# Mixture-of-experts stage: plain activations gathered, norm applied on gathered rows and products, nineteen weight places instead of sixteen

## The chip, the cores and the metric

The kernel runs on one core of a Trainium2 chip. The metric is the device time of one execution in microseconds (us); lower is better. TensorE (PE) multiplies matrices, VectorE (DVE) and ScalarE (ACT) work element by element, GpSimd (POOL) issues the gathers and scatters with indices, and SyncE (SP) issues the plain transfers.

## What is computed

The program is a network of three layers on 512 tokens of width 1024, all in float32. The change lies in the last stage, a mixture of experts: each token goes to two of 32 experts.

```python
h2 = rms_norm_2(x, g_ffn[l])
x = x + hier_moe(h2, ...)

def rms_norm_2(x, g):
    y = xf * lax.rsqrt(jnp.mean(xf * xf, axis=-1, keepdims=True) + EPS)
    return (y * g.astype(jnp.float32)).astype(x.dtype)

def hier_moe(h, wg, bg, we, be, w1, w3, w2):
    pg = softmax(hf @ wg + bg)           # 4 groups, the best one is taken
    le = (hf @ we + be)                  # 8 experts in it, the best two are taken
    ...
    def expert_block(args):
        xb, e = args
        return (jax.nn.silu(xb @ w1[e]) * (xb @ w3[e])) @ w2[e]
    ...
    ys = ys * gate_buf[:, None]
    out = zeros.at[tok_buf].add(ys)
```

`w1` and `w3` of an expert are 1024 x 512 each, `w2` is 512 x 1024: 6 MB for an expert, 192 MB for all of them. The root of a token's mean square is one number for a token, the gain `g_ffn` one number for a feature.

## The kernel before

The activations `x` and the normed `um` lie with features on partitions (8 tiles of 128 x 512). The stage needs rows of tokens, so it goes like this.

**Head.** While the last projection of the attention (`CH_2O`, lines 548 to 576) still runs, `act_sum` scales `x` by `g_ffn` into `um` on ACT (L1132). `pe_route` multiplies `um` by the router's weights (L2403) and sums the squares (L2399), PE turns `um` to token order (L2366), and ACT copies the turned tiles out with the token's root as scale (L2541). SP stores those rows to DRAM (`h_tokens`, L2336). DVE works out the routing (`dve_route`); for each expert `dve_slots` makes a 0/1 matrix (L2601), `pe_meta` multiplies it by a table of token numbers and gates (L2431), and `dve_indices` turns the result into indices (L2611 to L2613). Three experts' indices are made ahead (`AHEAD`).

**One round of the loop over experts.** PE's order is written out in `pe_expert(e)`: the up products of expert e (L2458, 16 matmuls of the program, which the profile shows as 32), the turn of the hidden rows of expert e-1 (L2490), the turn of the gathered rows of expert e+1 (`pe_x_turn`, L2450), the meta product of expert e+3 (L2431), the down products of expert e-1 (L2466). ACT works out the sigmoid in three steps (L2553 to L2557), copies the turned hidden rows (L2560), copies the turned gathered rows out of their bank (`act_gathered`, L2582) and scales the expert's output by its gate (L2590). DVE multiplies (L2631, L2633), makes the slots of expert e+3 (L2601), multiplies by the sigmoid (L2640), and makes the indices. POOL gathers the rows of expert e+3 when the turned bank lets it, and scatters the outputs. Each engine runs its own list in order; semaphores join them.

In rounds 4 to 7 PE also turns `x` itself to token order (`pe_tokens`, L2420) and ACT copies it out (`act_tokens`): the experts' outputs are added to it at the end.

**Weights.** An expert has six pieces of 128 x 2048 (1 MB). SP loads them in the order of use into 16 places (`SLOTS`). A piece can be issued when the piece 16 before it has been used (`w_used`). Nine places are free while the last projection runs; seven (`LATE`) lie where the ring of dense weights and other tiles are, and the last two are loaded behind the stores of `h_tokens`. After the last scatter but before the last two pieces SP loads the scattered pairs back (L2353), and the last three experts' outputs are put in place by products (`pe_last`, L2524; `dve_last`, L2676).

Of the kernel before, what the change touches and what calls it, by code (L numbers as in the profile page):

```python
# [36 lines left out]
SLOTS = 16  # L37
LAST = 3
LATE = 7
# [1059 lines left out]
def scalar_program(k):  # L1099
    act, s = k.act, k.s  # L1100
    k.nc.scalar.preload_act_table_set("natural_log_exp_and_others")
    act.wait_ge(s["gains_in"], 16)
    for j in range(4):
        act.wait_ge(s[f"x_in{j}"], 16)
        act_inputs(k, k.u, "g_a0", (2 * j, 2 * j + 1))
        for i in range(2):
            act_square_sum(k, 0, 2 * j + i, 2 * j + i)
    act.wait_ge(s["eps_ready"], 2)
    act_project(k, CH_AB, N_AB, k.y, lambda: act_root(k, "norm_a0", k.ch7, k.ch7.bank, k.rs, D))
    act_ab_prepare(k)  # L1110
# [12 lines left out]
    act_da(k)  # L1123
    act_sb(k)
    act_sum(k, CH_2O, 5, k.um, "g_ffn")
# [1094 lines left out]
def moe_buffers(k):  # L2220
    s = k.s
    k.dense.close()
    s.new("router_in", *(f"w_in{j}" for j in range(SLOTS) if j >= len(W_IN) and not 0 <= j - SLOTS + LATE < RING))
    s.new("routed", "route_shifted", "route_exp")
    s.new("h_turned", "h_copied0", "h_copied1", "h_stored", "x_turned", "x_copied0", "x_copied1")
# [17 lines left out]
    k.mt = [k.sb(f"mt{j}", [P, 4]) for j in range(2 * SETS)]  # L2243
# [12 lines left out]
    k.rtok = k.small[:, 480:496]  # L2256

# [36 lines left out]
W_IN = ("x_in0", "x_in1", "x_in2", "x_in3", "cmp_k_in", "cmp_v_in", "tables_in")  # L2294
# [6 lines left out]
def piece_in(k, j):  # L2301

    late = j - SLOTS + LATE
    if 0 <= late < RING:
# [16 lines left out]
def moe_sync(k):  # L2321
    sp, s = k.sp, k.s
    sp.wait_ge(s["o_normed"], 8)
    sp.dma_start(k.wr, k.t["router"]).then_inc(s["router_in"], 16)
    for g, (e, i) in enumerate(ORDER):
        if g == PAIRS_AT:
# [29 lines left out]
def moe_tensor(k):  # L2356
    pe, s = k.pe, k.s
    pe_route(k)
    for b in range(NB):
        for h in range(2):  # L2360
# [4 lines left out]
            for kk in range(4):  # L2365
                ins = pe.transpose(k.bank[4 + 2 * (b % 2) + h][:, kk * P:(kk + 1) * P], k.um[:, 4 * h + kk, b * P:(b + 1) * P], k.const("ident"))  # L2366
# [19 lines left out]
def pe_route(k):  # L2386
# [3 lines left out]
    pe.wait_ge(s["router_in"], 16)  # L2390
    for kk in range(KT):
        if kk == 0:
            pe.wait_ge(s["combined"], 2 * (N_CH // 2 - 1))
            pe.wait_ge(s["u_ready"], 46)
        if kk == KT - 2:
# [5 lines left out]
            pe.wait_ge(s["u_ready"], 48)  # L2401
        for b in range(NB):
            ins = pe.matmul(k.bank[b][:, 0:NG + NE], k.um[:, kk, b * P:(b + 1) * P], k.wr[:, kk, :], start=kk == 0, stop=kk == KT - 1)  # L2403
# [5 lines left out]
AHEAD, X_TURN = 3, 4  # L2409
TOKEN_BANKS = (3, 6)  # L2410


def pe_tokens(k, b):

    pe, s = k.pe, k.s
    for h in range(2):
        if b:
            pe.wait_ge(s[f"x_copied{h}"], b)
        for kk in range(4):
            ins = pe.transpose(k.bank[TOKEN_BANKS[h]][:, kk * P:(kk + 1) * P], k.x[:, 4 * h + kk, b * P:(b + 1) * P], k.const("ident"))  # L2420
        ins.then_inc(s["x_turned"], 1)


def pe_meta(k, e):
# [103 lines left out]
def moe_scalar(k):  # L2528
# [3 lines left out]
    act.wait_ge(s["root_ready"], k.root_at["norm_ffn"])  # L2532
    for b in range(NB):
# [5 lines left out]
        for h in range(2):  # L2539
            act.wait_ge(s["h_turned"], 2 * b + h + 1)  # L2540
            act.activation(k.htok[b][:, h * T:(h + 1) * T], k.bank[4 + 2 * (b % 2) + h], ACT.Copy,  # L2541
                           scale=k.rtok[:, 4 * b:4 * b + 1]).then_inc(s[f"h_copied{h}"], 1)
    act.wait_ge(s["h_stored"], 16 * NB)
    half = EH // 2
    sig = k.sig[:, 0:half]
    for e in range(NE + 1):
        if e == 0:
            act_gathered(k, 0)
        if e < NE:
            act.wait_ge(s["w_used"], up_used(e))  # L2550
            if e:
                act.wait_ge(s["hid_done"], e)
            act.activation(sig, k.bank[2][:, 0:half], ACT.Exp, scale=-1.0).then_inc(s["sig_exp"], 1)  # L2553
# [7 lines left out]
        if e + 1 < NE:  # L2561
            act_gathered(k, e + 1)
        if e:
            act_out(k, e - 1)
        if 0 <= e - X_TURN < NB:
            act_tokens(k, e - X_TURN)


def act_tokens(k, b):
    act, s = k.act, k.s  # L2570
    for h in range(2):
        act.wait_ge(s["x_turned"], 2 * b + h + 1)
        act.copy(k.xtok[:, b, h * T:(h + 1) * T], k.bank[TOKEN_BANKS[h]]).then_inc(s[f"x_copied{h}"], 1)

# [30 lines left out]
def dve_indices(k, e):  # L2605
# [5 lines left out]
    dve.wait_ge(own.sem, own.link(dve.tensor_copy(mt, k.bank[7][:, 0:4])))  # L2611
    dve.wait_ge(own.sem, own.link(dve.tensor_scalar(mt[:, 3:4], mt[:, 3:4], -4.0 * T, k.const("half_far"), ALU.mult, ALU.add)))
    dve.tensor_scalar(idx, mt[:, 0:2], 2.0, mt[:, 3:4], ALU.mult, ALU.add).then_inc(s["idx_ready"], 1)  # L2613
# [5 lines left out]
def moe_vector(k):  # L2619
# [5 lines left out]
    dve_count(k)  # L2625
    for e in range(NE):
# [16 lines left out]
        if e == NE - 2:  # L2643
            dve.wait_ge(s["x_copied0"], NB)
            dve.wait_ge(s["x_copied1"], NB)
# [42 lines left out]
def dve_route(k):  # L2688
# [19 lines left out]
    own.link(dve.memset(k.meta[:, :, :, 3], 1.0))  # L2708
# [57 lines left out]
def moe_pool(k):  # L2766
    pool, s = k.pool, k.s
    pool.wait_ge(s["zeroed"], 64)
# [25 lines left out]
def fallback(k, e, c):  # L2794
# [19 lines left out]
    gates = own.link(dve.tensor_copy(mt, k.bank[7][:, 0:4]))  # L2814
# [11 lines left out]
    act.wait_ge(s["f_pe"], done.link(ins))  # L2826
    act.copy(xT.rearrange("p c a t -> p (c a t)"), k.bank[0]).then_inc(s["f_act"], 1)
    pe.wait_ge(s["f_act"], 1)
# [3 lines left out]
    act.activation(sig, k.bank[2][:, 0:half], ACT.Exp, scale=-1.0).then_inc(s["f_act"], 1)  # L2832
    act.wait_ge(s["f_act"], 2)
    act.activation(sig, sig, ACT.Ln, bias=1.0).then_inc(s["f_act"], 1)
    act.wait_ge(s["f_act"], 3)
    act.activation(sig, sig, ACT.Exp, scale=-1.0).then_inc(s["f_act"], 1)
    dve.wait_ge(s["f_act"], 4)
    dve.wait_ge(own.sem, own.link(dve.tensor_tensor(k.prod, sig, k.bank[2][:, 0:half], ALU.mult)))
    hid = own.link(dve.tensor_tensor(hN, k.prod, k.bank[2][:, half:EH], ALU.mult))
# [5 lines left out]
    pe.wait_ge(s["f_act"], 5)  # L2845
# [41 lines left out]
```

## Time and profile before

| | |
|---|---|
| time, median of 3 runs | 2402.06 us |
| lowest and highest run | 2401.61 and 2406.68 us |
| span of the profiled execution | 2390.3 us |
| PE busy | 2240.4 us (94%) |
| DVE busy | 1375.2 us (58%) |
| ACT busy | 563.7 us (24%) |
| mean granted TensorE clock | 0.967 of full |

The span runs from the first to the last instruction of the profiled execution; the time of a run also holds what lies around it, some 11.8 us by the median. The stage of the experts begins with the first up product at 1888.4 us of the span. Its weights are read at some 418 GB/s, and PE is busy for some 91% of it. An engine's busy share says little here, since PE and the transfers both run nearly without a break; one has to see which of the two the other waits for.

### The profile page before, as it was taken

To read this page: it belongs to the slowest core of one execution; us is meant where nothing else is said; L and a number is where in the kernel's file an instruction comes from. 1 tells how busy PE (TensorE), PEld (TensorE's weight loads), DVE (VectorE), ACT (ScalarE), POOL (GpSimd) and SP (SyncE) were. 2 spreads that over 40 slices of the span, in tenths; PEclk is the share of its full clock that TensorE was granted. 3 is DMA by queue.
4 is the path that set the end of the run, shared out by engine and by line. 5 is a ranking of instruction groups with operands and counts; after the bars stand their busy time and mean duration, and the time that the engine had idled before them with its cause. 6 is when DMAs were issued, how large, how long until landed. Compare 5 with 4: busy or idle time off the path is not lost.

```text
span 2390.3 us, 29072 instructions
## 1 busy us (share of the span) xinstructions
PE 2240.4 (94%) x10734; PEld 1630.0 (68%) x10734; DVE 1375.2 (58%) x3525; ACT 563.7 (24%) x1375; POOL 64.7 (3%) x65
## 2 busy tenths in 40 slices
PE   8988889999999998999999999999799899899987
PEld 6864568888888885558888888888557533333332
DVE  6559857666566657996665666765776311211114
ACT  2013342100011205772100010301583211211110
POOL 0000000000000000000000000000000011111110
PEclk9998799999999999999999999999899799999999
DMA  5220022222323320002332222333004799999997
GB/s 201 88 80 7 17 72 73 87 87 88 88 89 88 126 64 25 1 1 71 88 87 86 85 88 85 100 88 88 1 1 179 276 418 414 418 417 417 418 418 297
DMA packets 69885, 348.11 MB, mean 146 GB/s; under 512 B 10852, under 2 KB 11748, under 8 KB 44208
## 3 DMA queue, kind: packets, MB, share of 16 engines
q1 hardware_dynamic: 64576, 337.13, 38.9%
q0 software_dynamic: 4880, 8.05, 0.9%
q8 instruction: 88, 1.44, 0.2%
q10 hardware_dynamic: 288, 1.05, 0.1%
q14 instruction: 53, 0.43, 0.1%
HBM read 341.00 MB, written 17.30 MB: 150 GB/s over the span
## 4 chain that ended last, share of the span: by engine, by line
PE 71%; DVE 8%; DMA 4%; ACT 3%; issue 2%; DVEq 0%; SPq 0%; ACTq 0%
PE bank L557 26%; PE bank L2458 8%; PE bank L562 7%; PE bank L576 7%; PE bank L569 7%; PE bank L2466 5%; DMA w<-in_experts 4%; PE bank L548 2%; PE bank L2431 1%; DVE exps L1806 1%; PE bank L889 1%; DVE square L2601 1%; PE bank L876 1%; PE bank L901 1%; DVE exps L1996 1%
## 5 line engine op out<-in xcount | busy, mean ns | idle before, releaser
L2458 PE MATMUL bank<-w,xT 128*64 128x512 f32 x960 | 215.6, 598 | 5.7 <-DMA w<-in_experts 4.9
L2631 DVE COPY square<-bank 128x256 f32<-128x256 f32 x32 | 13.6, 425 | 353.1 <-ACT rope L2553 353.1
L2458 PEld LDWEIGHTS bank<-w,xT 128*64 128x64 f32 x960 | 68.3, 138 | 145.4 <-issue 133.1
L1302 ACT ACTIVATE exps<-exps,small 128x128 f32<-128x128 f32 (+1 forms) x224 | 124.3, 559 | 100.2 <-DVE small L1806 99.7
L557 PE MATMUL bank<-u,ring 128*128 128x256 f32 x608 | 143.7, 379 | 0.0
L1576 DVE TENSOR_TENSOR third<-first,bank 128x256 f32<-128x256 f32 x108 | 45.5, 421 | 170.6 <-PE bank L557 169.8
L2466 PE MATMUL bank<-w,square 128*64 128x512 f32 x480 | 131.1, 695 | 5.8 <-ACT square L2560 2.9
L557 PEld LDWEIGHTS bank<-u,ring 128*128 128x128 f32 x608 | 115.4, 190 | 16.5 <-issue 1.0
L557 PE MATMUL bank<-h,ring 128*128 128x256 f32 x512 | 120.9, 379 | 0.0
L557 PE MATMUL bank<-h_sums,w_sum 128*128 128x256 f32 x512 | 120.9, 379 | 0.0
L557 PE MATMUL bank<-u_mlp_sums,w_sum 128*128 128x256 f32 x480 | 113.4, 379 | 0.0
L557 PE MATMUL bank<-u_mlp,ring 128*128 128x256 f32 x480 | 113.4, 379 | 0.0
L557 PE MATMUL bank<-exps,w_sum 128*128 128x256 f32 x464 | 109.6, 379 | 0.0
L557 PEld LDWEIGHTS bank<-h,ring 128*128 128x128 f32 x512 | 97.3, 190 | 13.2
L557 PEld LDWEIGHTS bank<-h_sums,w_sum 128*128 128x128 f32 x512 | 97.3, 190 | 13.2
L1243 ACT ACTIVATE h<-relu 128x512 f32<-128x512 f32 x64 | 40.3, 630 | 274.1 <-DVE relu L1721 249.3
L557 PEld LDWEIGHTS bank<-u_mlp,ring 128*128 128x128 f32 x480 | 91.2, 190 | 12.4
L557 PEld LDWEIGHTS bank<-u_mlp_sums,w_sum 128*128 128x128 f32 x480 | 91.2, 190 | 12.4
L557 PEld LDWEIGHTS bank<-exps,w_sum 128*128 128x128 f32 x464 | 88.2, 190 | 12.0
L2790 POOL DMA_INDIRECT x_gathered<-h_tokens,idx x32 | 35.3, 1103 | 2080.3 <-DVE idx L2613 1881.1
L2466 PEld LDWEIGHTS bank<-w,square 128*64 128x64 f32 x480 | 36.8, 157 | 75.8 <-issue 69.6
L2431 PE MATMUL bank<-sums,square 128*128 128x4 f32 x256 | 37.9, 271 | 48.7 <-DVE square L2601 48.7
(442 smaller groups left out, 4228.4 us busy)
## 6 DMA issues: line engine op xcount, KB each, us to landing
w<-in_experts SPq DMA_DIRECT2D x180, 1024.0 KB, 21.1
ring<-in_dense SPq DMA_DIRECT2D x216, 512.0 KB, 3.7
consts<-in_experts SPq DMA_DIRECT2D x12, 1024.0 KB
w<-y_pairs SPq DMA_DIRECT2D x4, 1024.0 KB, 26.8
consts<-in_consts SPq DMA_DIRECT2D x1, 2310.5 KB, 16.5
x<-in_xT SPq DMA_DIRECT2D x4, 512.0 KB, 8.0
h_tokens<-u SPq DMA_DIRECT2D x4, 512.0 KB, 2.8
bias_scratch<-y_ab SPq DMA_DIRECT2D x4, 320.0 KB, 2.4
```

What stands on the lines that cost most here:

```text
L548: ins = pe.matmul(bank, w[:, j, :], x(j), start=i == 0, stop=i == 3)
L557: ins = pe.matmul(bank, w[:, j, :], x(j), start=j == 0, stop=j == 3)
L562: ins = pe.matmul(part[2], a12[:, j, :], tile(2 * j + 1)[:, 0:HT], start=j == 0, stop=j == 3)
L569: ins = pe.matmul(part[4], a22[:, j, :], t4[:, j, :], start=j == 0, stop=j == 3)
L576: ins = pe.matmul(part[3], s4[:, j, :], tile(2 * j + 1)[:, HT:T], start=j == 0, stop=j == 3)
L1243: act.activation(k.hs[q % 2][:, j + a, :], k.rc[a], ACT.Square).then_inc(s["h_ready"], 1)
L1302: act.activation(e, e, ACT.Exp, bias=neg[:, a:a + 1], scale=-1.0, accum_out=total[:, a:a + 1]).then_inc(s[done], 1)
L1576: dve.tensor_tensor(u3, u2, part[7], ALU.add).then_inc(s["shared"], 1)
L2431: ins = pe.matmul(k.bank[7][:, 0:4], k.S[:, b, :], k.meta[:, b, e, :], start=b == 0, stop=b == NB - 1)
L2458: ins = k.pe.matmul(bank[a * CAP:(a + 1) * CAP, :], xT[:, kk % 4, kk // 4, :], w[:, (2 * (kk % 2) + a) * EH:(2 * (kk % 2) + a + 1) * EH], ...
L2466: ins = k.pe.matmul(bank[a * CAP:(a + 1) * CAP, :], hT[:, c % 2, c // 2, :], w[:, c % 2 * D + a * T:c % 2 * D + (a + 1) * T], start=c == 0 ...
L2790: k.pool.indirect_dma_start(k.xgat, None, k.hscr, bass.IndirectOffsetOnAxis(ap=k.idx[e % (2 * SETS)][:, 0:1].bitcast(U32), axis=0), bounds ...
```

## The change

The normed activations are no longer made. The router's weights are scaled by the gain instead, once, on POOL; the plain `x` is turned to token order, copied without a scale, stored and gathered. The gain is then applied by DVE when it copies the turned gathered rows out of their bank, and the root of each row by a scale on ACT and DVE where the products of the expert are read. The root comes with the row: the fourth column of the meta table, so far all ones, holds minus the root, and one more DVE instruction finds the empty slots. Since the plain rows now lie in token order from the start, the turns of `x` in rounds 4 to 7 go, and the tile `x` is free for weights behind the stores: two places. A third comes from halving the region where descriptors of POOL's transfers are kept (`SCRATCH`).

```diff
-SLOTS = 16
+SLOTS = 19
+EARLY, LATE = 12, 5
-LATE = 7
+SCRATCH = 8192
...
-    act_sum(k, CH_2O, 5, k.um, "g_ffn")
+    act_sum(k, CH_2O, 5, None, None)
...
-    late = list(range(SLOTS - LATE, SLOTS))
-    k.w = {j: k.sb(f"w{j}", [P, PIECE]) for j in late + list(range(SLOTS - LATE - 1))}
+    k.w = {j: k.sb(f"w{j}", [P, PIECE]) for j in [*range(EARLY, EARLY + LATE), *range(2, EARLY)]}
     done = k.cpack.at["swap"][0]
-    k.w[SLOTS - LATE - 1] = k.consts[:, done:done + PIECE]
+    k.w[1] = k.consts[:, done:done + PIECE]
+    for j in range(2):
+        k.w[EARLY + LATE + j] = k.x.rearrange("p k t -> p (k t)")[:, PIECE * j:PIECE * (j + 1)]
...
 def moe_sync(k):
     sp, s = k.sp, k.s
+    load_piece(k, *ORDER[0])
     sp.wait_ge(s["o_normed"], 8)
     sp.dma_start(k.wr, k.t["router"]).then_inc(s["router_in"], 16)
...
-        if g == SLOTS - LATE:
+        if g == EARLY:
             sp.wait_ge(s["prod_done"], 7 * N_CH // 2)
-        if g == SLOTS - 3:
+        if g == EARLY + LATE - 1:
             sp.wait_ge(s["combined"], N_CH)
-        if g == SLOTS - 2:
+        if g == EARLY + LATE:
...
     for e in range(NE + 1):
         pe_expert(k, e)
-        if 0 <= e - X_TURN < NB:
-            pe_tokens(k, e - X_TURN)
...
-            act.activation(sig, k.bank[2][:, 0:half], ACT.Exp, scale=-1.0).then_inc(s["sig_exp"], 1)
+            act.activation(sig, k.bank[2][:, 0:half], ACT.Exp, scale=minus_root(k, e)).then_inc(s["sig_exp"], 1)
...
-def act_gathered(k, e):
-    k.act.wait_ge(k.s["g_turned"], e + 1)
-    k.act.copy(k.xT[e % 2].rearrange("p c a t -> p (c a t)"), k.bank[0]).then_inc(k.s["g_copied"], 1)
+def dve_gathered(k, e):
+
+    gains = k.vec("g_ffn").rearrange("p (a c) -> p c a", a=2).unsqueeze(3).to_broadcast([P, 4, 2, CAP])
+    k.dve.wait_ge(k.s["g_turned"], e + 1)
+    k.dve.tensor_tensor(k.xT[e % 2], k.bank[0].rearrange("p (c a t) -> p c a t", c=4, a=2), gains, ALU.mult).then_inc(k.s["g_copied"], 1)
...
-    dve.wait_ge(own.sem, own.link(dve.tensor_scalar(mt[:, 3:4], mt[:, 3:4], -4.0 * T, k.const("half_far"), ALU.mult, ALU.add)))
-    dve.tensor_scalar(idx, mt[:, 0:2], 2.0, mt[:, 3:4], ALU.mult, ALU.add).then_inc(s["idx_ready"], 1)
+    dve.wait_ge(own.sem, own.link(dve.tensor_scalar(mt[:, 4:5], mt[:, 3:4], 0.0, -4.0 * T, ALU.is_lt, ALU.mult)))
+    dve.wait_ge(own.sem, own.link(dve.tensor_scalar(mt[:, 4:5], mt[:, 4:5], k.const("half_far"), None, ALU.add)))
+    dve.tensor_scalar(idx, mt[:, 0:2], 2.0, mt[:, 4:5], ALU.mult, ALU.add).then_inc(s["idx_ready"], 1)
...
+    dve_gathered(k, 0)
     for e in range(NE):
...
-        dve.tensor_copy(k.prod, k.bank[2][:, 0:half]).then_inc(s["taken"], 1)
+        dve.tensor_scalar(k.prod, k.bank[2][:, 0:half], minus_root(k, e), None, ALU.mult).then_inc(s["taken"], 1)
         dve.wait_ge(s["taken"], e + 1)
-        dve.tensor_tensor(k.prod, k.prod, k.bank[2][:, half:EH], ALU.mult).then_inc(s["both"], 1)
+        dve.scalar_tensor_tensor(k.prod, k.bank[2][:, half:EH], minus_root(k, e), k.prod, ALU.mult, ALU.mult).then_inc(s["both"], 1)
+        if e + 1 < NE:
+            dve_gathered(k, e + 1)
         if e + AHEAD < NE:
             dve_slots(k, e + AHEAD)
...
+    pool.wait_ge(s["router_in"], 16)
+    pool.tensor_tensor(k.wr, k.wr, k.vec("g_ffn").unsqueeze(2).to_broadcast([P, KT, NG + NE]), ALU.mult).then_inc(s["router_scaled"], 1)
```

The list of DVE, one round of the loop in the kernel before. `square_6` is the product, `square_7` the slots of expert e+3, `rope_9` the hidden rows, `mt` and `idx` the table row and the indices.

```order
2998 L2631 COPY square_6<-bank 128x256
2999 L2633 TENSOR_TENSOR square_6<-square_6,bank 128x256
3000 L2601 TENSOR_SCALAR square_7<-consts,pos 128x128 x4
3001 L2640 TENSOR_TENSOR rope_9<-square_6,rope_10 128x256
3002 L2611 COPY mt_98<-bank 128x4
3003 L2612 TENSOR_SCALAR mt_98<-mt_98,consts 128x1
3004 L2613 TENSOR_SCALAR idx_106<-mt_98 128x2
```

The same round in the changed kernel; `xT` are the turned gathered rows.

```order
3011 L2613 TENSOR_SCALAR square_6<-bank,mt_96 128x256
3012 L2615 SCALAR_TENSOR_TENSOR square_6<-bank,mt_96,square_6 128x256
3013 L2562 TENSOR_TENSOR xT_89<-bank,vecs 128x512
3014 L2581 TENSOR_SCALAR square_7<-consts,pos 128x128 x4
3015 L2624 TENSOR_TENSOR rope_9<-square_6,rope_10 128x256
3016 L2591 COPY mt_99<-bank 128x4
3017 L2592 TENSOR_SCALAR mt_99<-mt_99 128x1
3018 L2593 TENSOR_SCALAR mt_99<-mt_99,consts 128x1
3019 L2594 TENSOR_SCALAR idx_107<-mt_99 128x2
```

An operation of 512 elements a partition, so far ACT's, now stands on DVE between the second product and the slots, and the indices take four instructions instead of three.

The list of SP around the stores of `h_tokens` in the kernel before: the late places from `w_72` on, and behind the stores the last two before the places come round.

```order
260 L2312 DMA w_86<-in_experts 128x2048
261 L2312 DMA consts<-in_experts 128x2048
262 L2312 DMA w_72<-in_experts 128x2048
263 L2312 DMA w_73<-in_experts 128x2048
264 L2312 DMA w_74<-in_experts 128x2048
265 L2312 DMA w_75<-in_experts 128x2048
266 L2312 DMA w_76<-in_experts 128x2048
267 L2336 DMA h_tokens<-u 128x1024 x4
268 L2312 DMA w_77<-in_experts 128x2048
269 L2312 DMA w_78<-in_experts 128x2048
270 L2312 DMA w_79<-in_experts 128x2048
```

And in the changed kernel.

```order
263 L2315 DMA w_85<-in_experts 128x2048
264 L2315 DMA w_86<-in_experts 128x2048
265 L2315 DMA w_72<-in_experts 128x2048
266 L2315 DMA w_73<-in_experts 128x2048
267 L2315 DMA w_74<-in_experts 128x2048
268 L2315 DMA w_75<-in_experts 128x2048
269 L2315 DMA w_76<-in_experts 128x2048
270 L2342 DMA h_tokens<-u 128x1024 x4
271 L2315 DMA x<-in_experts 128x2048 x2
272 L2315 DMA w_131<-in_experts 128x2048
```

Twelve pieces instead of nine now stand ahead of the five late ones (`w_77` and `w_78` have moved up among them), and the two behind the stores go into `x`.

## Rows read from the trace of the kernel before

**Rows 1.** Stretches: busy PE, PEld, DVE, ACT, POOL (us); granted clock, DMA share, GB/s

```profile
1842.00:1855.00 13.00, 13.00 (x65) 11.50 (x63) 5.78 (x14) 3.32 (x6) 0.00 (x0) 1.00 0.09 38
...
1883.00:1891.00 8.00, 5.73 (x20) 3.45 (x22) 2.23 (x12) 0.58 (x1) 1.00 (x1) 0.50 0.12 32
...
2250.00:2360.00 110.00, 95.16 (x442) 35.85 (x442) 21.76 (x66) 18.18 (x42) 12.56 (x12) 0.97 1.01 418
```

**Rows 2.** Timeline of SP's transfers, the first behind the stores: start, length, engine, line

```profile
1874.06 23.76 SPq L2312 DMA_DIRECT2D w<-in_experts  x6
```

**Rows 3.** Timeline of PE late in the stage; in brackets idle time and releaser

```profile
2268.78 5.32 PE L2458 MATMUL bank<-w,xT 128*64 128x512 f32 x24
...
2276.38 0.44 PE L2490 MATMUL bank<-consts,rope 128*128 128x128 f32 x2
...
2283.70 3.60 PE L2458 MATMUL bank<-w,xT 128*64 128x512 f32 x16
...
2292.29 0.44 PE L2490 MATMUL bank<-consts,rope 128*128 128x128 f32 x2
...
2325.88 3.65 PE L2466 MATMUL bank<-w,square 128*64 128x512 f32 x16 [0.83 <-ACT square L2560]
...
2340.54 0.44 PE L2490 MATMUL bank<-consts,rope 128*128 128x128 f32 x2
...
2372.42 5.42 PE L2466 MATMUL bank<-w,square 128*64 128x512 f32 x16 [2.83 <-DMA w<-in_experts]
```

**Rows 4.** Timeline of one undisturbed round, from the end of its up products

```profile
2115.76 0.44 PE L2490 MATMUL bank<-consts,rope 128*128 128x128 f32 x2
...
2116.04 0.60 PE L2450 MATMUL bank<-consts,x_gathered 128*128 128x128 f32 x4
...
2116.85 0.42 DVE L2633 TENSOR_TENSOR square<-square,bank 128x256 f32<-128x256 f32 x1
...
2117.19 0.87 DVE L2601 TENSOR_SCALAR square<-consts,pos 128x128 f32<-128x128 f32 x4
2117.32 0.59 ACT L2582 COPY xT<-bank 128x512 f32<-128x512 f32 x1
...
2118.11 1.05 PE L2431 MATMUL bank<-sums,square 128*128 128x4 f32 x8 [1.48 <-DVE square L2601]
...
2119.10 3.65 PE L2466 MATMUL bank<-w,square 128*64 128x512 f32 x16
...
2122.58 7.04 PE L2458 MATMUL bank<-w,xT 128*64 128x512 f32 x32
2129.55 0.44 PE L2490 MATMUL bank<-consts,rope 128*128 128x128 f32 x2
```

**Rows 5.** Timeline of DVE, an operation of 512 elements and its successor

```profile
1795.57 0.68 DVE L2139 TENSOR_TENSOR y<-y 128x512 f32<-128x512 f32 x1
1796.17 0.68 DVE L2147 TENSOR_TENSOR y<-y,bank 128x512 f32<-128x512 f32 x1
```

**Rows 6.** The chain that ended last: start, length, what; down products and a token turn

```profile
1938.93 5.28 PE bank L2466 x16
1976.28 1.02 PE bank L2420 x8
2036.45 3.58 PE bank L2466 x16
2174.31 3.58 PE bank L2466 x16
2204.02 6.47 PE bank L2466 x16
```

**Rows 7.** Timeline ahead of the first up product: indices, count, copy

```profile
1886.99 0.21 DVE L2612 TENSOR_SCALAR mt<-mt,consts 128x1 f32<-128x1 f32 x1
1887.24 0.23 DVE L2613 TENSOR_SCALAR idx<-mt 128x2 int32<-128x2 f32 x1
...
1887.60 0.15 DVE L2763 CAST count<-col 128x1 int32<-128x1 f32 x1
```

More of the change, by code:

```diff
@@ L2222, in moe_buffers @@
     k.dense.close()
-    s.new("router_in", *(f"w_in{j}" for j in range(SLOTS) if j >= len(W_IN) and not 0 <= j - SLOTS + LATE < RING))
+    s.new("router_in", "router_scaled", *(f"w_in{j}" for j in range(len(W_IN), SLOTS) if not EARLY <= j < EARLY + LATE))
     s.new("routed", "route_shifted", "route_exp")
-    s.new("h_turned", "h_copied0", "h_copied1", "h_stored", "x_turned", "x_copied0", "x_copied1")
+    s.new("h_turned", "h_copied0", "h_copied1", "h_stored")
     s.new("counted_in", "counted", "count_ready")
@@ L2242, in moe_buffers @@
     k.oN = [k.sb(f"oN{j}", [P, D // 2]) for j in range(SETS)]
-    k.mt = [k.sb(f"mt{j}", [P, 4]) for j in range(2 * SETS)]
+    k.mt = [k.sb(f"mt{j}", [P, 5]) for j in range(2 * SETS)]
     k.idx = [k.sb(f"idx{j}", [P, 2], I32) for j in range(2 * SETS)]
@@ L2256, in moe_buffers @@
     k.rtok = k.small[:, 480:496]
+    k.w[0] = k.sb("w0", [P, PIECE])
 def moe(k):
@@ L2301, in piece_in @@
 def piece_in(k, j):
-    late = j - SLOTS + LATE
-    if 0 <= late < RING:
+    late = j - EARLY
+    if 0 <= late < LATE:
         return k.s[f"ring_in{late}"], 16 * ((N_CH - late + RING - 1) // RING)
@@ L2389, in pe_route @@
     pe, s, ch = k.pe, k.s, k.ch7
-    pe.wait_ge(s["router_in"], 16)
+    pe.wait_ge(s["router_scaled"], 1)
     for kk in range(KT):
@@ L2400, in pe_route @@
             ch.end(ins, "norm_ffn")
-            pe.wait_ge(s["u_ready"], 48)
+            pe.wait_ge(s["combined"], N_CH)
         for b in range(NB):
-            ins = pe.matmul(k.bank[b][:, 0:NG + NE], k.um[:, kk, b * P:(b + 1) * P], k.wr[:, kk, :], start=kk == 0, stop=kk == KT - 1)
+            ins = pe.matmul(k.bank[b][:, 0:NG + NE], k.x[:, kk, b * P:(b + 1) * P], k.wr[:, kk, :], start=kk == 0, stop=kk == KT - 1)
     ins.then_inc(s["routed"], 1)
[L2409 to L2421, printed above, removed]
+AHEAD = 3
 def pe_meta(k, e):
@@ L2540, in moe_scalar @@
             act.wait_ge(s["h_turned"], 2 * b + h + 1)
-            act.activation(k.htok[b][:, h * T:(h + 1) * T], k.bank[4 + 2 * (b % 2) + h], ACT.Copy,
-                           scale=k.rtok[:, 4 * b:4 * b + 1]).then_inc(s[f"h_copied{h}"], 1)
-    act.wait_ge(s["h_stored"], 16 * NB)
+            act.copy(k.htok[b][:, h * T:(h + 1) * T], k.bank[4 + 2 * (b % 2) + h]).then_inc(s[f"h_copied{h}"], 1)
     half = EH // 2
@@ L2707, in dve_route @@
     own.link(dve.tensor_copy(k.meta[:, :, :, 0], tok))
-    own.link(dve.memset(k.meta[:, :, :, 3], 1.0))
+    own.link(dve.tensor_scalar(k.meta[:, :, :, 3], k.rtok[:, 0:4 * NB:4].unsqueeze(2).to_broadcast([P, NB, NE]), -1.0, None, ALU.mult))
     dve.wait_ge(s["routed"], 1)
@@ L2813, in fallback @@
     dve.wait_ge(s["f_pe"], done.link(ins))
-    gates = own.link(dve.tensor_copy(mt, k.bank[7][:, 0:4]))
+    gates = own.link(dve.tensor_copy(mt[:, 0:4], k.bank[7][:, 0:4]))
     for b in range(NB):
@@ L2825, in fallback @@
                                 start=b == 0, stop=b == NB - 1)
-    act.wait_ge(s["f_pe"], done.link(ins))
-    act.copy(xT.rearrange("p c a t -> p (c a t)"), k.bank[0]).then_inc(s["f_act"], 1)
-    pe.wait_ge(s["f_act"], 1)
+    gains = k.vec("g_ffn").rearrange("p (a c) -> p c a", a=2).unsqueeze(3).to_broadcast([P, 4, 2, CAP])
+    dve.wait_ge(s["f_pe"], done.link(ins))
+    pe.wait_ge(s["f_dve"], own.link(dve.tensor_tensor(xT, k.bank[0].rearrange("p (c a t) -> p c a t", c=4, a=2), gains, ALU.mult)))
     for kk in range(KT):
@@ L2831, in fallback @@
     act.wait_ge(s["f_pe"], done.link(ins))
-    act.activation(sig, k.bank[2][:, 0:half], ACT.Exp, scale=-1.0).then_inc(s["f_act"], 1)
+    act.wait_ge(s["f_dve"], gates)
+    act.activation(sig, k.bank[2][:, 0:half], ACT.Exp, scale=mt[:, 3:4]).then_inc(s["f_act"], 1)
+    act.wait_ge(s["f_act"], 1)
+    act.activation(sig, sig, ACT.Ln, bias=1.0).then_inc(s["f_act"], 1)
     act.wait_ge(s["f_act"], 2)
-    act.activation(sig, sig, ACT.Ln, bias=1.0).then_inc(s["f_act"], 1)
-    act.wait_ge(s["f_act"], 3)
     act.activation(sig, sig, ACT.Exp, scale=-1.0).then_inc(s["f_act"], 1)
-    dve.wait_ge(s["f_act"], 4)
-    dve.wait_ge(own.sem, own.link(dve.tensor_tensor(k.prod, sig, k.bank[2][:, 0:half], ALU.mult)))
-    hid = own.link(dve.tensor_tensor(hN, k.prod, k.bank[2][:, half:EH], ALU.mult))
+    dve.wait_ge(s["f_act"], 3)
+    dve.wait_ge(own.sem, own.link(dve.scalar_tensor_tensor(k.prod, k.bank[2][:, 0:half], mt[:, 3:4], sig, ALU.mult, ALU.mult)))
+    hid = own.link(dve.scalar_tensor_tensor(hN, k.bank[2][:, half:EH], mt[:, 3:4], k.prod, ALU.mult, ALU.mult))
     pe.wait_ge(s["f_dve"], hid)
```

39 lines of the change are left out of this document (13 added, 26 removed).

## The prediction

> **What bounds the kernel now.** I read the stretches of time first [rows 1]. From the first experts to the end the transfers run without a break at 418 GB/s (DMA share 1.01), and in the same 110 us PE is busy for 95.16. So both are close to their limit, and the question is which waits for which. There are two paths through the stage, and the end is the later of them.
>
> The path of the transfers: a piece of 128 x 2048 float32 is 1.0486 MB, at 418 GB/s 2.51 us. The transfers can only run ahead as far as there are places. Before the first up product they stood still twice: from 1842 to 1855 the share is 0.09, all nine early places being full, and from 1883 to 1891 it is 0.12, all sixteen being full [rows 1].
>
> The path of PE: in an undisturbed round the up products begin at 2122.58 and end where the next turn begins, at 2129.55, after 6.97 us [rows 4]. A round that waits for weights shows as a longer stretch between those two. Late in the stage there are three: 2268.78 to 2276.38 is 7.60, so 0.63 lost; 2283.70 to 2292.29 is 8.59, so 1.62 lost; and the products that follow the down products begun at 2325.88 should start after 3.48 us (2119.10 to 2122.58 [rows 4]), at 2329.36, and end at 2340.54, 11.18 later, so 4.21 lost. The last down products wait 2.83 [rows 3]. Sum 9.3 us: without any wait for weights PE would have ended at 2390.3 - 9.3 = 2381.0. That is all the slack it has. Until some 2270 us the bound is PE, and only the last seven rounds see the transfers.
>
> **The change, part by part.** All sums are made against the profiled span of 2390.3 us; the median of the runs is 11.8 us above it, which I add at the end.
>
> *Three more places.* Three pieces that were read behind the first up product are now read in the pause from 1842 to 1855, which is long enough for three (7.5 us of 13), and the two behind the stores are issued at 1874.06 as before [rows 2], so that all nineteen are full when the first is used. The path of the transfers gets 3 x 2.51 = 7.5 us shorter.
>
> *No normed copy, no scale on the copy of the turned tiles.* ACT's work in the head shrinks. It gives nothing: the first gather waits for indices, which hang on the routing, not on ACT. The router's weights are scaled on POOL, which is idle there, some 30 us before they are read.
>
> *Ahead of the first up product.* The indices take one more instruction, 0.25 us each time (1886.99 to 1887.24 [rows 7]), and three experts' indices are made in a row there: 0.75. The gathered rows used to be copied by ACT at 1887.80; now DVE does it behind the count, which ends at 1887.75, plus 0.75 is 1888.50, plus 0.68 for 512 elements [rows 5] is 1889.2. The first up product, at 1888.44 before, starts 0.8 later. Both paths carry that.
>
> *One round.* This is the term that matters. In the round shown, PE turns the gathered rows from 2116.04 to 2116.64 and then stands idle for 1.48 us, because the meta product needs the slots, which DVE makes from 2117.19 to 2118.06, behind its two products. ACT's copy of the gathered rows, 0.59 us from 2117.32 on, lies beside that and costs nothing [rows 4]. In the changed kernel DVE does this copy itself, in front of the slots. Its input is there (2116.64) before the second product ends (2117.27), so nothing hides it: slots, meta product, down products and next up products all move by one DVE operation of 512 elements. The distance from such an operation to the next one is 0.60 us, its own length 0.68 [rows 5]; I take 0.60, with 0.68 for the range. Below zero it cannot go, since an operation is added in front and none of DVE's goes; the two products only change their form. Of the 32 rounds 29 make slots: 29 x 0.60 = 17.4 us (19.7 at 0.68). The fourth index instruction falls beside the down products and costs nothing, and so does the hidden product (L2640), which is late by 0.6 but has the whole of the next up products in front of it.
>
> *The turns of x go.* Four times 1.02 us of PE [rows 6]: 4.1 less. ACT's copies lay beside PE and cost nothing.
>
> *PE's clock.* Most down products take 3.58 us, some 5.28 or 6.47 [rows 6]. Of the 32 pieces of down products in the chain ten are longer than 5 us, from the one at 1938.93 [rows 6] to the one at 2372.42 [rows 3]; these are the rounds in which the granted clock goes from full (2.4 GHz) to half (1.2 GHz), after the stretch in which PE only turns, waits and multiplies by four columns. That stretch, from the end of the up products (2115.76) to the start of the down products (2119.10), is 3.3 us now [rows 4] and will be 3.9. A fall costs 5.28 - 3.58 = 1.7 us, or 2.9 in a double one. The falls come in groups: from 2036.45 to 2174.31 eleven rounds in a row have none [rows 6], with three and three close together on either side. So it depends on where the stretch lies against something that runs by itself, and rounds of 13.8 us keep step with it for a while; rounds of 14.4 will not. With the stretch a fifth longer I take half of the rounds instead of a third, six more, at 1.7: 10.2 us. The ends are none, and every round.
>
> *The region for descriptors.* It is halved. No row shows it. POOL's 61 gathers and scatters carry little, and each is waited for a whole round later, so I take nothing; the price of a stall would have to be over 5 us each time to show.
>
> **The sums.** Transfers: 2390.3 - 7.5 + 0.8 = 2383.6. PE: 2381.0 + 0.8 + 17.4 - 4.1 = 2395.1 with as many falls as now, and with six more 2405.3. PE's path is the later one, so the three places buy nothing. In run time: 2405.3 + 11.8 = 2417.1.
>
> **The rivals.**
>
> *The transfers decide, and the change gains.* For it: the last seven rounds before do wait for weights, and share 1.01 says that there is no slack. Against it: PE has 9.3 us in hand and is asked for 14.1 already without a change of the clock. It needs an added delay of less than (2383.6 - 2381.0 - 0.8 + 4.1) / 29 = 0.20 us a round, so DVE's copy would have to be hidden for the most part, or the falls would have to become fewer by the same 11 us. Time 2383.6 + 11.8 = 2395.4, faster by 6.7 us.
>
> *PE decides, but the clock falls as often as now.* For it: the longer stretch is longer by 0.6 us only. Time 2395.1 + 11.8 = 2406.9, just slower. It decides against the forecast if ten or eleven long down products are counted again.
>
> *The clock falls in every round.* 22 more falls at 1.7 are 37 us: 2395.1 + 37.4 + 11.8 = 2444. For it: a stretch of 3.9 us without large products. Against it: stretches of 3.3 us go without a fall in two rounds of three, and 0.6 us is no great step. The Trainium skill is on the side of this rival: "TensorE: Matmul & The Clock Gate" (section "HAM oscillation — how this bites in real kernels") tells of a kernel whose clock fell behind every gap between two groups of matmuls, and asks for work without such gaps. The trace agrees in part only, with ten falls behind 32 gaps [rows 3, 6]; by the rule the sum is this rival's 2444, by the rows the forecast.
>
> *The places bring nothing because they are not filled in time.* If the stores and the two pieces behind them are late, the path of the transfers is between 2383.6 and 2391.1. This doesn't change the forecast, since PE ends later than either.
>
> **How the numbers follow.** PE decides with more falls: 0.56, the forecast, 2417, from 2410 (two more) to 2425 (eight more, some double, or 0.68 a round). PE decides with falls as now, 2403 to 2410: 0.22. The transfers decide, 2393 to 2399: 0.14. Falls in nearly every round or a stall of the gathers, above 2427: 0.08. The range 2400 to 2427 leaves out the third and the fourth. A difference of 0.2%, 4.8 us, is about what a measurement can tell from none: between 2397.3 and 2406.9 nothing is to be told. Faster: most of the third case, 0.12. The same: half of the second and the rest of the third, 0.13. Slower: 0.75.
>
> **What would show it.** In the profile of the changed kernel: the first up product at some 1889; twelve pieces read by some 1848 instead of nine by 1842; PE's idle time before the meta product 2.1 us instead of 1.5, released by the slots; undisturbed rounds of 14.4 us instead of 13.8; some sixteen down products of over 5 us; nearly no wait of PE for `in_experts`, and for the first time pauses in the transfers within the stage, with SP waiting for PE. Wrong it would be if the slots stood no later than now, if the copy on DVE took part of the time that the sigmoid leaves free, or if at the end PE still waited for weights in many rounds.

## The result and the profile after

The changed kernel takes 2457.2 us (median of 5 runs, 2436.2 to 2459.6) against 2401.6 us for the kernel before (5 runs, 2391.7 to 2406.7). The ratio is 1.022, with a 95% interval of 1.020 to 1.025: slower by 2.2%, or 56 us. The time lies 30 us above the stated range, which ended at 2427.

The span of the profiled execution is 2446.9 us. Its own time was 2448.3, so what lies around a span is 1.4 us. The 11.8 us of the prediction, and of the section on the time before, were something else: the part of the program ahead of the experts takes one of two lengths. In the ten profiles of this document the first up product comes at 1888 to 1891 us of the span six times, and at 1898 to 1900 four times. The profiled execution of the kernel before, a span of 2390.3 and so a time of some 2391.7, was a short one; the three runs stated beside it, from 2401.6 up, were long ones. So what follows compares the **stage**, from the first up product to the end of the span: 2390.3 - 1888.4 = 501.9 us before, 2446.9 - 1888.8 = 558.1 after, 56.2 more. All of the loss lies in it.

The stretches of the changed kernel (columns as in rows 1: busy PE, PEld, DVE, ACT, POOL, then granted clock, DMA share, GB/s):

```profile
1842.00:1855.00 13.00, 13.00 (x65) 11.51 (x64) 5.96 (x14) 1.52 (x3) 0.00 (x0) 1.00 0.64 265
1883.00:1891.00 8.00, 5.39 (x20) 3.45 (x22) 3.13 (x15) 0.00 (x0) 0.99 (x1) 0.50 0.11 32
```

The pause of the transfers at 1842 is put to use (share 0.64 instead of 0.09 [rows 1]), and at 1883 all places, now nineteen, are full again. The three places do what they should. Then the long middle of the stage, first before, then after:

```profile
1950.00:2350.00 400.00, 355.71 (x1689) 140.95 (x1686) 70.73 (x263) 75.40 (x170) 55.06 (x52) 0.95 1.01 417
```

```profile
1950.00:2350.00 400.00, 345.15 (x1462) 136.99 (x1460) 81.98 (x277) 52.50 (x116) 47.86 (x47) 0.85 0.98 383
```

The transfers no longer run at their limit (383 GB/s instead of 417, share 0.98), and PE does fewer matmuls (1462 instead of 1689) in nearly the same busy time, at a granted clock of 0.85 of full. In the kernel before PE waited 7.7 us for weights in the stage; now it has no such wait left, and waits for DVE. From its waits (engine, line, what it waits for, us in total, times, longest; three of the 32 lie ahead of the stage):

```profile
PE bank L2422 <- DVE square L2581: 75.0, 32, 2.5
```

One round of the changed kernel, from the end of its up products (timeline; it answers to rows 4):

```profile
2230.74 0.44 PE L2478 MATMUL bank<-consts,rope 128*128 128x128 f32 x2
2230.86 0.47 ACT L2537 ACTIVATE rope<-bank,mt 128x256 f32<-128x256 f32 x1 [6.18 <-PE bank L2446]
...
2231.02 0.60 PE L2438 MATMUL bank<-consts,x_gathered 128*128 128x128 f32 x4
...
2231.47 0.48 DVE L2613 TENSOR_SCALAR square<-bank,mt 128x256 f32<-128x256 f32 x1 [11.90 <-ACT rope L2537]
...
2231.99 0.48 DVE L2615 SCALAR_TENSOR_TENSOR square<-bank,mt,square 128x256 f32<-128x256 f32 x1
...
2232.39 0.68 DVE L2562 TENSOR_TENSOR xT<-bank,vecs 128x512 f32<-128x512 f32 x1
...
2232.98 0.96 DVE L2581 TENSOR_SCALAR square<-consts,pos 128x128 f32<-128x128 f32 x4
...
2234.00 1.87 PE L2422 MATMUL bank<-sums,square 128*128 128x4 f32 x8 [2.38 <-DVE square L2581]
...
2235.80 5.89 PE L2454 MATMUL bank<-w,square 128*64 128x512 f32 x16
```

The meta product starts 3.26 us behind the up products (2230.74 to 2234.00); before it was 2.35 (2115.76 to 2118.11 [rows 4]). That is 0.91 more, of which the copy in front of the slots (2232.39 to 2232.98) is 0.59. For the rest two more lines of the round in rows 4 are needed, from the kernel before:

```profile
2115.88 0.38 ACT L2553 ACTIVATE rope<-bank 128x256 f32<-128x256 f32 x1 [6.18 <-PE bank L2458]
2116.39 0.42 DVE L2631 COPY square<-bank 128x256 f32<-128x256 f32 x1 [10.29 <-ACT rope L2553]
```

The sigmoid's first step, now with a scale for each row, takes 0.47 us instead of 0.38, and each of the two products 0.48 instead of 0.42: 0.21 together. The slots take 0.96 instead of 0.87, though their instruction is the same; why is not shown.

And the chain of the same stretch, in which three rounds follow each other:

```profile
2199.87 1.87 PE bank L2422 x8
2201.74 5.81 PE bank L2454 x16
2207.55 6.89 PE bank L2446 x32
...
2217.61 1.05 PE bank L2422 x8
2218.66 5.28 PE bank L2454 x16
2223.94 6.89 PE bank L2446 x32
...
2234.00 1.87 PE bank L2422 x8
2235.86 5.82 PE bank L2454 x16
2241.68 6.89 PE bank L2446 x32
```

The down products (L2454) take 5.28 and 5.8 us in turn instead of the 3.58 of rows 6, and in every second round the meta product (L2422) too takes 1.87 instead of 1.05. Rounds last 16.4 and 17.7 us (up products at 2207.55, 2223.94, 2241.68), 34.13 for the pair, and this goes on from 1945 to the round at 2320. Of the 28 rounds that have both a meta and a down product only the first is undisturbed; 27 have a fall, where the kernel before had ten in all. Without a fall a round would be 13.79 + 0.91 = 14.70, two of them 29.4. So the falls cost 34.13 - 29.4 = 4.7 us in two rounds, 2.4 us each.

That it is the clock, stretches of half a microsecond of the same round show (columns as above):

```profile
2231.50:2232.00 0.50, 0.12 (x2) 0.00 (x0) 0.46 (x2) 0.47 (x2) 0.00 (x0) 1.00 0.98 410
...
2233.00:2233.50 0.50, 0.00 (x0) 0.00 (x0) 0.50 (x4) 0.00 (x0) 0.47 (x1) 1.00 0.93 393
2233.50:2234.00 0.50, 0.00 (x1) 0.00 (x1) 0.50 (x4) 0.00 (x0) 0.00 (x0) 0.51 1.09 459
...
2240.00:2240.50 0.50, 0.50 (x4) 0.24 (x2) 0.00 (x0) 0.00 (x0) 0.00 (x0) 0.66 0.28 115
2240.50:2241.00 0.50, 0.50 (x4) 0.14 (x2) 0.00 (x0) 0.00 (x0) 0.00 (x0) 1.00 1.24 197
```

PE did the two turns and stood idle from 2231.6 on; at 2233.5 the granted clock went from 1.00 to 0.50, and it came back at some 2240.3. In the round before this one it fell later, at 2219.9, within the down products.

One more sum shows why this decides. An expert's six pieces take 6 x 2.51 = 15.1 us to read. Rounds of 13.8 and 14.7 us are shorter than that: PE uses the pieces a little faster than they are read and lives on those read ahead. Rounds of 16.4 and 17.7 us are longer, and the transfers wait for PE.

### The profile page after: what moved, and what is told of

It is laid out like the page before. It is cut to its first block, busy times and chain, and to the rows that moved or that the text cites. A ratio compares the mean times of both kernels' runs of the same rounds, so it can differ in the third digit from the quotient of the medians.

```text
span 2446.9 us, 29030 instructions
## 1 busy us (share of the span) xinstructions
PE 2274.9 (93%) x10702; PEld 1644.0 (67%) x10702; DVE 1404.8 (57%) x3589; ACT 541.2 (22%) x1327; POOL 63.1 (3%) x66
## 3 DMA queue, kind: packets, MB, share of 16 engines
q10 hardware_dynamic: 288, 1.05, 0.1%
## 4 chain that ended last, share of the span: by engine, by line
PE 73%; DVE 9%; ACT 3%; issue 2%; DVEq 0%; ACTq 0%
PE bank L558 25%; PE bank L2446 9%; PE bank L563 7%; PE bank L577 7%; PE bank L570 7%; PE bank L2454 7%; PE bank L549 2%; PE bank L2422 2%; DVE exps L1807 1%; DVE square L2581 1%; PE bank L890 1%; PE bank L877 1%; PE bank L902 1%; DVE exps L1997 1%; ACT rope L2537 1%
## 5 line engine op out<-in xcount | busy, mean ns | idle before, releaser
L2613 DVE TENSOR_SCALAR square<-bank,mt 128x256 f32<-128x256 f32 x32 | 15.5, 484 | 372.2 <-ACT rope L2537 372.2
L2446 PE MATMUL bank<-w,xT 128*64 128x512 f32 x872 | 196.9, 601 | 0.9 <-DVE xT L2562 0.9
L2446 PEld LDWEIGHTS bank<-w,xT 128*64 128x64 f32 x872 | 62.5, 139 | 129.9 <-issue 128.7
L2454 PE MATMUL bank<-w,square 128*64 128x512 f32 x424 | 140.1, 820 | 1.9 <-ACT square L2544 1.9
L2422 PE MATMUL bank<-sums,square 128*128 128x4 f32 x256 | 45.9, 303 | 75.0 <-DVE square L2581 75.0
L2422 PEld LDWEIGHTS bank<-sums,square 128*128 128x128 f32 x256 | 43.2, 255 | 82.3 <-DVE square L2581 79.6
L2454 PEld LDWEIGHTS bank<-w,square 128*64 128x64 f32 x424 | 38.6, 186 | 80.0 <-issue 77.3
```

The source lines that it names most:

```text
L2422: ins = pe.matmul(k.bank[7][:, 0:4], k.S[:, b, :], k.meta[:, b, e, :], start=b == 0, stop=b == NB - 1)
L2446: ins = k.pe.matmul(bank[a * CAP:(a + 1) * CAP, :], xT[:, kk % 4, kk // 4, :], w[:, (2 * (kk % 2) + a) * EH:(2 * (kk % 2) + a + 1) * EH], ...
L2454: ins = k.pe.matmul(bank[a * CAP:(a + 1) * CAP, :], hT[:, c % 2, c // 2, :], w[:, c % 2 * D + a * T:c % 2 * D + (a + 1) * T], start=c == 0 ...
```

## The experiments

The theory after the result: DVE's delay of 0.9 us a round by itself is nearly harmless; it stretches the part of PE's round that has no large products, the granted clock then falls in nearly every round, and that is where the time goes. The rivals: the transfers have become slower in themselves; or the delay costs what it is long; or the places do harm. Where a length of the stage is given, it is from the profiled execution, first up product to the end of the span: one execution, so not always the typical one. Ratios are to runs of the kernel before made beside each version, whose median was 2400.5 us (29 runs) beside the first four and 2395.9 (22 runs) beside the last four, since each set mixes the two lengths of the part ahead.

### The two DVE operations exchanged

```diff
+        if e + AHEAD < NE:
+            dve_slots(k, e + AHEAD)
         if e + 1 < NE:
             dve_gathered(k, e + 1)
-        if e + AHEAD < NE:
-            dve_slots(k, e + AHEAD)
```

> The changed kernel with one edit: DVE makes the slots first and multiplies the gathered rows by the gain behind them, so the slots come 0.6 us earlier in each round (the meta product some 2.65 us behind the end of the up products; 2.35 in the kernel before, 3.26 in the changed one). Theory (the operation in front of the slots delays PE by 0.9 us a round, and the longer stretch with little for PE to multiply makes the granted clock fall in every round): undisturbed rounds of 14.1 us, falls in some 12 to 20 of the 32 rounds instead of nearly all, 2395 to 2415 us, where the changed kernel has 2436 to 2459. Rival (the transfers are slower in themselves, 385 GB/s instead of 418, through the halved region for descriptors or the weights that lie in x, and PE is held up by them): the transfers stay at some 385 GB/s and the time stays above 2430.

Measured: median 2401.9 us, ratio to the kernel before 1.001 (0.999 to 1.003), some 55 us less than the changed kernel. Stage 2415.1 - 1900.1 = 515.0, but the profiled execution was the slowest of ten (2391.6 to 2416.4 us). With either length of the part ahead, the median run has a shorter stage, of some 500 or 512 us. The meta product starts 2.81 us behind the up products:

```profile
2105.45 0.44 PE L2478 MATMUL bank<-consts,rope 128*128 128x128 f32 x2
...
2107.10 1.10 DVE L2581 TENSOR_SCALAR square<-consts,pos 128x128 f32<-128x128 f32 x4
...
2108.26 1.87 PE L2422 MATMUL bank<-sums,square 128*128 128x4 f32 x8 [1.93 <-DVE square L2581]
```

In the chain the down products go in a pattern of six rounds (6.07, 3.58, 3.58, 5.28, 3.58, 5.28), so half of the rounds have a fall. The transfers are back at 418 GB/s between 1950 and 2350, with the halved region for descriptors and weights in `x` in place. The rival of slow transfers falls.

### The slots made before the round's products

The slots of expert e+3 need nothing of round e. DVE stands idle for some 12 us at the head of each round, and now makes them there.

```diff
     for e in range(NE):
+        if e + AHEAD < NE:
+            dve_slots(k, e + AHEAD)
         dve.wait_ge(s["w_used"], up_used(e))
...
         if e + 1 < NE:
             dve_gathered(k, e + 1)
-        if e + AHEAD < NE:
-            dve_slots(k, e + AHEAD)
```

> The changed kernel with the slots of expert e+3 made at the head of DVE's round, ahead of its wait for the up products, where DVE stands idle for some 12 us. Theory: the meta product no longer waits, PE's stretch without large products shrinks from 4.3 us to some 2, hardly any falls behind it, rounds of some 12.3 us as long as weights are there; from the moment the nineteen places are used up the transfers decide, at 418 GB/s, and the three places count: span 2383 to 2387, time 2384 to 2388, under both kernels. Rival (slow transfers): 385 GB/s and over 2430.

Measured: median 2388.5 us (12 runs, 2383.2 to 2393.8), ratio to the kernel before 0.996 (0.994 to 0.998): the lowest median of all versions, under both kernels, and half a microsecond above what was expected. Stage 2392.5 - 1899.8 = 492.7. The meta product follows the turn without a wait, and the engine that PE waits for is now the DMA, as this piece of its timeline shows:

```profile
2104.43 0.44 PE L2478 MATMUL bank<-consts,rope 128*128 128x128 f32 x2
2104.70 0.60 PE L2438 MATMUL bank<-consts,x_gathered 128*128 128x128 f32 x4
2105.14 0.95 PE L2422 MATMUL bank<-sums,square 128*128 128x4 f32 x8
2106.22 1.94 PE L2454 MATMUL bank<-w,square 128*64 128x512 f32 x8
2107.99 1.89 PE L2454 MATMUL bank<-x,square 128*64 128x512 f32 x8
2110.12 1.94 PE L2446 MATMUL bank<-x,xT 128*64 128x512 f32 x8 [0.24 <-DMA x<-in_experts]
2112.89 1.94 PE L2446 MATMUL bank<-w,xT 128*64 128x512 f32 x8 [0.84 <-DMA w<-in_experts]
```

The row of the middle of the stage has full clock and full transfers:

```profile
1950.00:2350.00 400.00, 342.07 (x1666) 126.69 (x1664) 88.34 (x307) 60.84 (x135) 53.42 (x53) 1.00 1.01 418
```

### The kernel before, with only the copy on DVE

```diff
-            act_gathered(k, e + 1)
...
+        if e + 1 < NE:
+            dve_gathered(k, e + 1)
         if e + AHEAD < NE:
             dve_slots(k, e + AHEAD)
```

Here `dve_gathered` is a plain copy; the root and the gain stay where they were.

> The kernel before with one part of the change alone: the copy of the turned gathered rows goes from ACT to DVE, in front of the slots (a plain copy, no gain, no root; sixteen places, turns of x in place). Theory: the meta product starts 0.6 to 0.7 us later in each round (some 3.0 us behind the up products), and the granted clock falls in most rounds: 2415 to 2450. Rival (this operation costs only its own 0.6 us a round, beside 9 us of slack): 2400 to 2410. Rival (slow transfers from the other parts of the change): as the kernel before, 2392 to 2407.

Measured: median 2421.8 us, ratio 1.010 (1.007 to 1.013). Stage 2411.0 - 1890.0 = 521.0, 19.1 more than the kernel before. From the timeline of one of its rounds:

```profile
2209.86 0.44 PE L2490 MATMUL bank<-consts,rope 128*128 128x128 f32 x2
2209.97 0.38 ACT L2551 ACTIVATE rope<-bank 128x256 f32<-128x256 f32 x1 [6.18 <-PE bank L2458]
...
2211.28 0.68 DVE L2578 COPY xT<-bank 128x512 f32<-128x512 f32 x1
...
2212.80 1.05 PE L2431 MATMUL bank<-sums,square 128*128 128x4 f32 x8 [2.07 <-DVE square L2597]
2213.79 5.35 PE L2466 MATMUL bank<-w,square 128*64 128x512 f32 x16
```

The copy moves the meta product by 0.59 us (2.94 behind the up products instead of 2.35), the term of the prediction. 29 x 0.59 = 17.1 less 9.3 of slack would be 8 us; it is 19. In this round the down products take 5.35 us, and from 2059 to 2320 about every second round has such a fall, where the kernel before has eleven rounds in a row without one. So a third of the loss goes with this one operation and its falls, and the other two thirds come with the last 0.3 us of delay a round.

### The changed kernel, with PE kept busy

```diff
-AHEAD = 3
+AHEAD, FILL = 3, 2
...
+    if e + AHEAD < NE - LAST:
+        for _ in range(FILL):
+            pe.matmul(k.bank[3], k.const("ident"), k.const("rope_c"), start=True, stop=True)
     if e + AHEAD < NE:
         pe_meta(k, e + AHEAD)
```

> The changed kernel with two filler matmuls (128x512 out of constants into a bank that nobody reads) between the turn of the gathered rows and the meta product, in rounds 0 to 25. At full clock they fit in the 2.4 us in which PE waits for the slots, so they take nothing away of the delay by DVE and only give PE something to do. Theory: the falls go nearly all (they cost some 1.7 us and 3.1 us in turn, 70 us together), rounds of 14.7 us, and the time comes down to 2385 to 2395. Rival (what counts is the delay on DVE alone, or the transfers): the time stays at 2436 to 2459 or gets longer.

Measured: median 2390.1 us, ratio to the kernel before 0.997 (0.995 to 0.999). Stage 2396.7 - 1898.6 = 498.2, 59.9 less than the changed kernel, with two useless products in 26 rounds and nothing taken from DVE. From a round of it:

```profile
2109.37 0.44 PE L2478 MATMUL bank<-consts,rope 128*128 128x128 f32 x2
...
2110.08 1.88 PE L2484 MATMUL bank<-consts 128*128 128x512 f32 x4
...
2112.63 1.05 PE L2422 MATMUL bank<-sums,square 128*128 128x4 f32 x8 [0.67 <-DVE square L2584]
2113.61 3.65 PE L2454 MATMUL bank<-w,square 128*64 128x512 f32 x16
```

The meta product starts as late as in the changed kernel (3.26 us behind the up products), but the down products are at 3.6 us again; two of the chain's pieces are longer than 5 us, in the last rounds, which have no filler. PE has no wait for weights in this run. This is the run that settles the matter: with the whole delay and nearly without falls the change would have been a small gain. Against the 56.2 us of loss stand 59.9 us that the falls cost.

### The kernel before, with only the slots early

```diff
     for e in range(NE):
+        if e + AHEAD < NE:
+            dve_slots(k, e + AHEAD)
...
-        if e + AHEAD < NE:
-            dve_slots(k, e + AHEAD)
```

> The kernel before (normed rows gathered, copy on ACT, sixteen places) with only the slots moved to the head of DVE's round. Lengths are given for the stage, from the first up product to the end of the span, since the part ahead of it takes one of two lengths, some 11 us apart, in every kernel: 501.9 us before, 558.1 changed, 492.7 with slots early in the changed kernel. Theory: without the wait the transfers decide here too, and with sixteen places their path is three pieces longer: 7.5 us more than the changed kernel with early slots, stage 499 to 502, so nearly nothing against the kernel before (which had 9 us of waits for weights and nothing to win from PE). Rival (the plain rows and the missing turns make the difference, not the places): the stage is 493 here as well. Second rival (PE with fewer falls gains by itself): under 496.

Measured: median 2392.0 us against 2395.9 for the kernel before, ratio 0.999 (0.997 to 1.001). Stage 2389.4 - 1888.2 = 501.2, as long as before to 0.7 us. PE does its rounds faster and then waits for weights, 60 us in all against 7.7 before. With sixteen places the transfers set this length.

### Early slots, with sixteen places

The fastest version with `SLOTS = 16` and `EARLY, LATE = 9, 5`; three tiles of its weights are left unused.

> The changed kernel with early slots and the three places undone (sixteen places, the region for descriptors still halved, two of the places still in x, three tiles left unused). Theory (the transfers decide once PE doesn't, and each piece read ahead is worth 2.5 us): stage 7.5 us longer than with nineteen, 499 to 502. Rival (the places are not what gives the gain): 492 to 494.

Measured: stage 2398.7 - 1898.1 = 500.6, so 7.9 us longer than with nineteen places (492.7). Three times 2.51 us are 7.5. Median 2400.0 us, ratio 1.001 (0.999 to 1.003).

### The changed kernel, with sixteen places

The same edit on the changed kernel itself.

> The changed kernel with only the three places undone. Theory (PE decides through the whole stage, and waits for no piece): as the changed kernel, stage 553 to 563, time 2436 to 2460. Rival (the places, or more transfers in flight, slow something down): clearly shorter, under 545.

Measured: stage 2448.9 - 1890.7 = 558.2, the same as with nineteen to 0.1 us; median 2459.1 us, ratio 1.027 (1.024 to 1.030). As long as PE decides, the places are worth nothing and do no harm.

### The kernel before, with only a delay

```diff
+        if e + AHEAD < NE:
+            at = k.cpack.at["rope_c"][0]
+            src = k.consts[:, at:at + 809]
+            dve.wait_ge(k.dve_own.sem, k.dve_own.n)
+            k.dve_own.link(dve.tensor_reduce(k.col[1][:, 0:1], src, AX.X, ALU.max))
         if e + AHEAD < NE:
             dve_slots(k, e + AHEAD)
```

> The kernel before with a useless operation of DVE (a reduction over 809 elements of constants, some 0.9 us) in front of the slots in each of 29 rounds, and nothing else of the change: the delay by itself at the size that the changed kernel shows (meta product 3.26 us behind the up products instead of 2.35). Theory: undisturbed rounds of 14.7 us, the granted clock falls in nearly every round, in turn for one and for two stretches (rounds of 16.4 and 17.8 us), stage 555 to 565 and the time 2440 to 2465. Rival (delay without more falls): 29 x 0.9 less 9 us of slack, stage 518 to 522, time 2408 to 2422.

Measured: median 2447.4 us, ratio 1.023 (1.019 to 1.026), which is the changed kernel's ratio. Stage 2440.1 - 1888.5 = 551.6.

```profile
2326.64 0.44 PE L2490 MATMUL bank<-consts,rope 128*128 128x128 f32 x2
...
2328.06 0.99 DVE L2638 TENSOR_REDUCE col<-consts 128x1 f32<-128x809 f32 x1
...
2329.90 1.86 PE L2431 MATMUL bank<-sums,square 128*128 128x4 f32 x8 [2.39 <-DVE square L2601]
...
2332.65 5.41 PE L2466 MATMUL bank<-w,square 128*64 128x512 f32 x16
```

The same 3.26 us (2326.64 to 2329.90), the same half clock in the meta and the down products, and nothing else of the change in it. The stage is 6.5 us shorter than the changed kernel's and 3 short of what was expected: in the first half some of its rounds have no fall, and the even pattern sets in only later.

In one table, by how far the meta product starts behind the up products:

| kernel | us behind the up products | stage, us | median ratio |
|---|---|---|---|
| changed, slots early | no wait | 492.7 | 0.996 |
| before | 2.35 | 501.9 | 1 |
| changed, operations exchanged | 2.81 | 515.0 | 1.001 |
| before, copy on DVE | 2.94 | 521.0 | 1.010 |
| before, delay alone | 3.26 | 551.6 | 1.023 |
| changed | 3.26 | 558.1 | 1.022 |
| changed, with filler | 3.26 | 498.2 | 0.997 |

From 2.35 to 3.26 the stage grows by 50 to 56 us, twice what 29 rounds x 0.91 us (26 us) could explain; with the filler the growth is gone. The stages are of single executions. That of the exchanged operations comes from its slowest run, and one run of the changed kernel, at 2436.2 us, was 12 us shorter than the profiled one.

## Why the prediction was right or wrong

*The three places:* right in size and in worth. They take 7.9 us off the path of the transfers (7.5 forecast), and nothing off the kernel while PE decides.

*Ahead of the first up product:* forecast at 1889.2, measured at 1888.8.

*PE decides:* right, and for the forecast reason, DVE's copy in front of the slots. The copy costs 0.59 us a round (0.60 forecast). What was mis-sized is the claim that the two products "only change their form": a factor for each row makes the sigmoid's first step and both products longer, by 0.21 us, and the slots take 0.1 more for a reason not shown. The delay is 0.91 instead of 0.60 us a round, which makes 9 us.

*PE's clock:* this is the step that failed. It saw the mechanism, and then took half of the rounds by a guess from the rows, six more falls at 1.7 us, 10.2 us together. In the run 27 rounds had a fall instead of ten, in the long even stretch at 2.4 us each. With the prediction's other terms and the measured delay the stage would be 501.9 - 9.3 + 29 x 0.91 - 4.1 = 514.9; it was 558.1, so the clock took some 43 us more than before, four times the 10.2. The step from "every round" to "half of the rounds" rested on 0.6 us being "no great step"; 0.3 us took the stage from 521.0 to 551.6 in the kernel before. The rival for it had the chance of 0.08 together with a stall and was priced at 2444; the run gave 2448 for the profiled execution. That this is near 2444 is luck: the price had single falls only, and 11.8 us of it were the wrong offset. As a span it was 2432.5, against 2446.9. The rows showed that the falls come in groups and the text even said that a round of other length would no longer keep step with what runs by itself. The opposite was seen: fall and lengthened round repeated as pairs of 34.13 us. Why they repeat is not shown.

*The slack of PE:* no run measured the 9.3 us by itself. The profile's own waits of PE for weights add up to 7.7, and behind the last one (2.83) the down products ran at half clock, which the sum left in. In the kernel before too some rounds had a fall, and that cost it nearly nothing: the early slots, which let PE do its rounds faster, win 0.7 us there, as the transfers were next.

*The offset of 11.8 us* was wrong, as shown above; it is 1.4 us, and the rest is the length of the part ahead. A single profile could not show it; the stated span, 11 us and more below every run listed beside it, was the hint. Added to a sum made from a short execution it gave a long one, and it went into the time of every rival.

*What would show it:* the first up product, the pause filled, the slots as the releaser and no wait for weights came as listed, and the transfers slowed to 383 GB/s with SP waiting for PE. SP waited for PE in the kernel before too (259 us of the 400 from 1950 on, 353 in the changed kernel), so that this would be seen "for the first time" was wrong. PE's idle time before the meta product was 2.4 us, not 2.1. Undisturbed rounds of 14.4 us did not come: there was one, of 14.67. Down products of over 5 us were 27, not sixteen. "Of the 32 pieces of down products in the chain" is not exact either: 26 lie on the chain, ten of them long, and the other six are short in the timeline.

## What to carry to other kernels

When an operation moves to an engine that another one waits for, ask not only for its own length but for what the waiting engine does meanwhile: a TensorE that pauses a little longer in each round can lose its full clock in each round, and that cost 60 us here, where the delays alone left a stage of 498.2 us, some 4 shorter than before the change. Cheap cures were to make the awaited input a round earlier, where the engine idles anyway, or to fill the wait with useless matmuls. Deeper prefetch pays only once the transfers decide; test it together with the fix for the other path, or it looks like a loss.

## What the runs showed of the hardware

That the granted clock can lock into a periodic pattern with the program was not expected. The changed kernel's rounds alternate between 16.4 and 17.7 us for some 375 us, the exchanged one's repeat after six rounds, the kernel before has eleven clean rounds in a row. The same delay of 0.91 us gave a stage of 558.1 us in one kernel and 551.6 in another. The Trainium skill ("TensorE: Matmul & The Clock Gate", "HAM oscillation — how this bites in real kernels") describes such a loss in every repetition of a loop for waits on transfers; here a wait for VectorE did the same. Ahead of each fall in the even stretch PE had done its turns and waited some 2.4 us for the slots, and in every second round it had also multiplied by four columns for 1.05 us and begun the down products. With two matmuls of 512 columns put into that wait, none of the 25 rounds with a down product that had them showed a fall.

The part ahead of the stage also has clock falls of its own, and its two lengths, some 10 us apart, go with different places of these falls: between 300 and 350 us the granted clock is 0.96 to 0.98 in the six profiles with the short part and 0.87 to 0.89 in the four with the long one. What picks the one or the other in an execution was not tried and stays open. Halving the region for the descriptors of indexed transfers had no cost that any of these runs shows: with it, the transfers reached 418 GB/s.
